# A hybrid attention and mixture-of-experts step: the last expert pair's rows are summed in PSUM, and the gathers go ahead of them

## The reference

```python
expert_id = g_sel[:, None] * EXPERTS_PER_GROUP + top_i          # two experts per token
gates = jnp.sum(jax.nn.one_hot(expert_id, N_EXPERTS) * top_w[..., None], axis=1)
a = jnp.einsum('nd,edf->nef', ht, w_gate)
u = jnp.einsum('nd,edf->nef', ht, w_up)
y = jnp.einsum('nef,efd->nd', jax.nn.silu(a) * u * gates[:, :, None], w_down)
x = layer_norm(ALPHA * x + gate * y, w, b)                      # gate: a row of the modulation
```

## Time and profile before

| what | us |
|---|---|
| median of 3 runs (1205.51 to 1209.25) | 1208.18 |
| the profiled execution's own time | 1204.98 |
| its span | 1203.1 |
| TensorE matmuls busy (fp32; two records for each) | 1047.1 (87%) |
| VectorE busy | 432.8 (36%) |
| ScalarE busy | 209.3 (17%) |
| POOL busy | 181.7 (15%) |
| mean granted TensorE clock | 0.928 |

### The profile page before, as it was taken

The page is one execution under the profiler, slowest core; times in us unless marked ns, Lnnn a source line. Parts: engine busy times, 40 slices in busy tenths (PEclk is TensorE's granted clock), DMA queues, the critical chain, the costliest instruction groups (busy, mean ns, idle before and its releaser), DMA issues.

```text
span 1203.1 us, 16527 instructions
## 1 busy us (share of the span) xinstructions
PE 1047.1 (87%) x6588; PEld 699.1 (58%) x6589; DVE 432.8 (36%) x1016; ACT 209.3 (17%) x524; POOL 181.7 (15%) x176
## 2 busy tenths in 40 slices
PE   4899999989979999887729999999896999998840
PEld 1766878568655555554328567775685655555420
DVE  0034545257741212100164344443686212211117
ACT  0322334100111111101102232421001111111000
POOL 0441020051111111101113000201312111111001
PEclk8899999999879999989859999999995999999985
DMA  8997222685999999999869312237858899999961
GB/s 353 249 270 238 70 84 71 226 293 241 348 419 418 419 419 419 418 420 419 331 210 320 106 67 80 103 112 281 320 213 340 332 416 419 419 418 419 412 260 60
DMA packets 102993, 343.83 MB, mean 286 GB/s; under 512 B 20530, under 2 KB 61538, under 8 KB 70404
## 3 DMA queue, kind: packets, MB, share of 16 engines
q1 hardware_dynamic: 88832, 316.58, 68.9%
q0 software_dynamic: 12352, 16.74, 4.6%
q10 hardware_dynamic: 1732, 9.45, 2.0%
HBM read 341.92 MB, written 26.16 MB: 306 GB/s over the span
## 4 chain that ended last, share of the span: by engine, by line
PE 69%; DMA 17%; DVE 4%; issue 4%; POOL 3%; ACT 2%; SPq 1%; POOLq 0%; DVEq 0%; ACTq 0%
PE ps L980 16%; PE ps L1254 15%; PE ps L973 8%; PE ps L1157 7%; PE ps L1278 7%; DMA ring<-in_exp_w_gate 5%; PE ps L1226 3%; DMA tables<-in_exp_w_gate 3%; DMA small<-in_exp_w_down 2%; DMA ring<-in_exp_w_down 2%; DMA ring<-in_w_mod 2%; PE ps L922 1%; PE ps L1073 1%; DMA arena<-token_rows,arena 1%; PE ps L1219 1%
## 5 line engine op out<-in xcount | busy, mean ns | idle before, releaser
L1254 PE MATMUL ps<-ring,arena 128*64 128x256 f32 x1488 | 211.0, 401 | 14.8 <-DMA ring<-in_exp_w_up 8.6
L980 PE MATMUL ps<-ring,arena 128*128 128x256 f32 (+1 forms) x960 | 200.1, 367 | 5.8 <-ACT arena L1488 5.8
L980 PEld LDWEIGHTS ps<-ring,arena 128*128 128x128 f32 x960 | 170.3, 195 | 28.7 <-issue 8.6
L1254 PEld LDWEIGHTS ps<-ring,arena 128*64 128x64 f32 x1488 | 129.7, 144 | 67.0 <-issue 26.2
L2050 DVE TENSOR_TENSOR arena<-arena,ps 128x256 f32<-128x256 f32 x32 | 13.5, 421 | 248.6 <-PE ps L1254 141.2
L973 PE MATMUL ps<-arena,ring 128*128 128x384 f32 x288 | 96.9, 490 | 0.7 <-ACT arena L1493 0.5
L1278 PE MATMUL ps<-ring,arena 128*64 128x512 f32 x304 | 80.3, 598 | 10.8 <-DMA ring<-in_exp_w_down 7.3
L1157 PE MATMUL ps<-ring,arena 128*128 128x256 f32 x384 | 87.9, 391 | 0.0
L1157 PEld LDWEIGHTS ps<-ring,arena 128*128 128x128 f32 x384 | 75.4, 198 | 10.8
L2236 POOL DMA_INDIRECT arena<-token_rows,arena x32 | 33.4, 1044 | 274.9 <-PE ps L1226 150.1
L1254 PE MATMUL ps<-arena 128*64 128x256 f32 x320 | 73.3, 382 | 1.9 <-DMA ring<-in_exp_w_up 1.7
(11 more groups left out here) (268 smaller groups left out, 1331.7 us busy)
## 6 DMA issues: line engine op xcount, KB each, us to landing
ring<-in_exp_w_up SPq DMA_DIRECT2D x51, 1024.0 KB, 24.2
ring<-in_exp_w_gate SPq DMA_DIRECT2D x46, 1024.0 KB, 22.6
ring<-in_w_mod SPq DMA_DIRECT2D x45, 1024.0 KB, 5.5
ring<-in_exp_w_down SPq DMA_DIRECT2D x40, 1024.0 KB, 27.3
ring<-in_w_in SPq DMA_DIRECT2D x24, 1024.0 KB, 13.3
arena<-in_exp_w_down SPq DMA_DIRECT2D x10, 1024.0 KB, 25.0
arena<-in_exp_w_gate SPq DMA_DIRECT2D x10, 1024.0 KB, 23.8
arena<-in_exp_w_up SPq DMA_DIRECT2D x10, 1024.0 KB, 25.2
```

Source lines behind the costliest of these rows:

```text
L980: mm = pe.matmul(out[:, 0:w], hT[:, ch, where * P:(where + 1) * P], unit(l, name)[:, ch, 0:w], start=(ch == 0), stop=(ch == CH - 1))
L1254: mm = pe.matmul(ps[64 * w:64 * w + 64, 2 * (i % 2) + kind, 0:FF], xgT[i % 2][:, ch, w * SLOTS:(w + 1) * SLOTS], weights[:, ch * FF:(ch + ...
```

## The change

- **Order.** Down 14 moves from after up 15 to directly after the turn of hidden 14, ahead of pair 15. Its weights move in the same way, and then come `gate2`, the last down weights, and `ln2`. The `gath` units reserve three ring places for the gathers.
- **Pair 15 is not scattered.** Its 128 rows are multiplied with the gate row on the way out of PSUM (`gate_last`), and TensorE adds them to the tokens with a matrix of gate weights (`marks_of_last`, `add_last`). `gate_weights` makes those weights and sets the weights of gathered rows that were not scattered to zero. The DRAM table is filled with zeros once, in layer 0, by eight POOL transfers of 384 KB.
- **Gathers.** ScalarE issues them during pair 15, once the scatters up to pair 14 have landed. ScalarE scales the first row and VectorE does the rest, alpha times x included (`add_choices`). TensorE copies this sum into PSUM (`add_former`).
- **Items** are single experts with 128 slots instead of pairs with 64, so three weight units are loaded instead of six. Their rows are not scattered either, but added in PSUM. An item starts after the last pair's rows have been read out.
- **The norm** takes its statistics and its first pass from PSUM. The moments of the tiles run ahead of the last passes.

```diff
 USE_ORDER = []
 for _i in range(PAIRS):
     USE_ORDER += [("pair", _i, _kind, _w) for _kind in range(2) for _w in range(2)]
-    if _i:
+    if _i and _i < PAIRS - 1:
         USE_ORDER += [("pair", _i - 1, 2, _w) for _w in range(2)]
-USE_ORDER += [("pair", PAIRS - 1, 2, _w) for _w in range(2)]
+    if _i == PAIRS - 2:
+        USE_ORDER += [("pair", _i, 2, _w) for _w in range(2)]
+LAST_DOWN = [("pair", PAIRS - 1, 2, _w) for _w in range(2)]
+GATH = [("gath", _t) for _t in range(TILES)]
+USE_ORDER += LAST_DOWN
+EXPERT_LOADS = USE_ORDER[:-2] + [("late", "gate2")] + GATH + LAST_DOWN + [("late", "ln2")]
+EXPERT_RELEASES = USE_ORDER[:-2] + GATH + LAST_DOWN + [("late", "gate2"), ("late", "ln2")]
...
-                if l:
-                    for t in range(TILES):
-                        sp.wait_ge(gathered[t].sem, gathered[t].at(l - 1, 16))
                 small_loads(l)
...
+                    if unit[0] == "late":
+                        load_late(l, unit[1])
+                    elif unit[0] != "gath":
+                        load(l, unit)
                 wait_alone(sp, items_known, items_known.at(l, 1))
                 o1 = items_before(sp, l + 1)
                 o0 = items_before(sp, l)
                 with sp.If(o1 > o0):
                     with sp.Fori(o0, o1) as i:
                         load_item(l, o0, i)
-                late_loads(l)
...
+                            if i == PAIRS - 1 and n == 1 and j == 0 and w == 0:
+                                mm.then_inc(down_half.sem, 1)
...
+            def add_former(l, t):
+
+                pe.wait_ge(presummed.sem, presummed.at(l, t + 1))
+                for n in range(2):
+                    pe.matmul(ps[:, FINAL_BANKS[t][n], :], ident, x[:, t, 512 * n:512 * n + 512], start=True, stop=False)
+
+            def add_last(l, t):
+
+                pe.wait_ge(last_rows.sem, last_rows.at(l, 1 + min(t, 1)))
+                for n in range(2):
+                    mm = pe.matmul(ps[:, FINAL_BANKS[t][n], :], ptl[:, t, :], ybg[min(t, 1)][:, 512 * n:512 * n + 512],
+                                   start=False, stop=True)
+                mm.then_inc(final_ready.sem, 1)
...
-                    if i:
+                    if i and i < PAIRS - 1:
                         down(l, i - 1)
 ...
                     hidden_T(l, i)
+                    if i == PAIRS - 2:
+                        down(l, i)
+                    if i == LAST_STEP:
+                        marks_of_last(l)
...
+                pe.wait_ge(last_rows.sem, last_rows.at(l, 2))
+                pe.wait_ge(o_rows.sem, o_rows.at(i, 0))
                 pe.wait_ge(o_xr_in.sem, o_xr_in.at(i, 16 * (l + 1)))
-                pe.wait_ge(xt_dve.sem, xt_dve.at(l, PAIRS))
-                turn_half(xr[0], 0).then_inc(o_xt.sem, 1)
+                turn_half(xr[0], 0, 6).then_inc(o_xt.sem, 1)
+                pe.wait_ge(o_gw.sem, o_gw.at(i, 1))
+                turn_marks([ps[:, 5, t * P:(t + 1) * P] for t in range(TILES)]).then_inc(o_pt.sem, 1)
...
+                for t in range(TILES):
+                    pe.wait_ge(o_rows.sem, o_rows.at(i, 1 + min(t, 1)))
+                    for n in range(2):
+                        mm = pe.matmul(ps[:, FINAL_BANKS[t][n], :], pti[t], yig[min(t, 1)][:, 512 * n:512 * n + 512],
+                                       start=False, stop=False)
+                mm.then_inc(o_added.sem, 1)
...
+                add_former(l, 0)
+                add_former(l, 1)
                 down(l, PAIRS - 1)
+                add_former(l, 2)
                 with pe.If(o1 > o0):
                     with pe.Fori(o0, o1) as i:
                         item(l, o0, i)
+                for t in range(TILES):
+                    add_last(l, t)
 
...
+            def load_rows_back(l):
+
+                for k in range(2):
+                    wait_alone(act, rows_out[k], rows_out[k].at(l, rows_out[k].step))
+                for t in range(TILES):
+                    wait_released(act, *SPOT[l, ("gath", t)][2])
+                    act.dma_start(gath(l, t).rearrange("p k d -> p (k d)"),
+                                  rows[1 + 2 * t * P:1 + 2 * (t + 1) * P].rearrange("(p k) d -> p (k d)", k=2))\
+                        .then_inc(gathered[t].sem, 16)
+
+            def weigh_first(l, t):
+
+                act.wait_ge(gathered[t].sem, gathered[t].at(l, 16))
+                a = gath(l, t)[:, 0, :]
+                act.activation(a, a, ACT.Identity, scale=wtsm[:, 0, t:t + 1]).then_inc(scaled.sem, 1)
...
-                    if i:
+                    if i and i < PAIRS - 1:
                         rows_half(l, i - 1)
+                    if i == PAIRS - 1:
+                        load_rows_back(l)
                     copy_hidden_T(l, i)
+                    if i == PAIRS - 2:
+                        rows_half(l, i)
+                    if i == LAST_STEP:
+                        marks_of_last(l)
                 wait_alone(act, items_known, items_known.at(l, 1))
                 o1 = items_before(act, l + 1)
                 o0 = items_before(act, l)
-                rows_half(l, PAIRS - 1)
+                act.wait_ge(weights_masked.sem, weights_masked.at(l, 1))
+                for t in range(TILES):
+                    weigh_first(l, t)
                 with act.If(o1 > o0):
                     with act.Fori(o0, o1) as i:
                         item(l, i)
 
...
+                for n, half in enumerate(sums_of(t)):
+                    cols = slice(512 * n, 512 * n + 512)
+                    ins = dve.scalar_tensor_tensor(xt[:, cols], half, ln_s[:, t, 12:13], lnw[:, cols], ALU.subtract, ALU.mult)
+                chain.link(ins)
...
+            def gate_weights(l, chain):
...
+            def marks_of_last(l, chain):
...
+            def add_choices(l, t, chain):
+
+                a, b = gath(l, t)[:, 0, :], gath(l, t)[:, 1, :]
+                dve.wait_ge(scaled.sem, scaled.at(l, t + 1))
+                chain.link(dve.scalar_tensor_tensor(a, b, wtsm[:, 1, t:t + 1], a, ALU.mult, ALU.add))
+                chain.link(dve.tensor_tensor(a, a, late_tile(l, "gate2", min(t, 1)), ALU.mult))
+                dve.scalar_tensor_tensor(x[:, t, :], x[:, t, :], ALPHA, a, ALU.mult, ALU.add).then_inc(presummed.sem, 1)
+
+            def gate_last(l):
+
+                dve.wait_ge(rows_out[0].sem, rows_out[0].at(l, rows_out[0].step))
+                dve.wait_ge(rows_out[1].sem, rows_out[1].at(l, rows_out[1].step))
+                dve.wait_ge(down_half.sem, down_half.at(l, 1))
+                gate = [late_tile(l, "gate2", k) for k in range(2)]
+                dve.tensor_tensor(ybg[0][:, 0:512], ps[:, 5, :], gate[0][:, 0:512], ALU.mult)
+                dve.wait_ge(down_ready.sem, down_ready.at(l, PAIRS))
+                dve.tensor_tensor(ybg[0][:, 512:D], ps[:, 6, :], gate[0][:, 512:D], ALU.mult).then_inc(last_rows.sem, 1)
+                dve.tensor_tensor(ybg[1].rearrange("p (a b) -> p a b", a=2), ps[:, 5:7, :],
+                                  gate[1].rearrange("p (a b) -> p a b", a=2), ALU.mult).then_inc(last_rows.sem, 1)
+
+            def final_moments(l, t, chain):
+
+                dve.wait_ge(final_ready.sem, final_ready.at(l, t + 1))
+                for n, half in enumerate(sums_of(t)):
+                    ins = dve.bn_stats(ln_s[:, t, 6 * n:6 * n + 6], half)
+                spread(t, chain, var2, ins)
...
+                        gate_weights(l, chain)
+                        dve.wait_ge(weights_masked.sem, weights_masked.at(l, 1))
+                        marks_of_last(l, chain)
                 o1 = items_before(dve, l + 1)
                 o0 = items_before(dve, l)
-                rows_half(l, PAIRS - 1)
+                dve.wait_ge(gate2_in.sem, gate2_in.at(l, gate2_in.step))
+                for t in range(TILES):
+                    add_choices(l, t, chain)
+                gate_last(l)
                 with dve.If(o1 > o0):
                     with dve.Fori(o0, o1) as i:
                         item(l, o0, i)
-                for t in range(TILES):
-                    dve.wait_ge(gathered[t].sem, gathered[t].at(l, 16))
-                    a, b = gath[t][:, 0, :], gath[t][:, 1, :]
-                    if t == 0:
-                        dve.wait_ge(gate2_in.sem, gate2_in.at(l, gate2_in.step))
-                    chain.link(dve.tensor_scalar(a, a, wts[:, 0, t:t + 1], None, ALU.mult))
-                    chain.link(dve.scalar_tensor_tensor(a, b, wts[:, 1, t:t + 1], a, ALU.mult, ALU.add))
-                    dve.tensor_tensor(a, a, late_tile(l, "gate2", min(t, 1)), ALU.mult).then_inc(combined.sem, 1)
-                    dve.wait_ge(combined.sem, combined.at(l, t + 1))
-                    chain.link(dve.scalar_tensor_tensor(x[:, t, :], x[:, t, :], ALPHA, a, ALU.mult, ALU.add))
-                    moments(t, chain, var2)
-                    normalise(l, t, chain)
+                dve.wait_ge(o_added.sem, o_added.at(o1, 0))
```

(15 more changed lines are left out.)

359 lines of the change are left out of this document (190 added, 169 removed).

## The result

The changed kernel takes **1214.51 us** (median of 6 runs, 1211.49 to 1217.07) against 1207.93 before (6 runs beside them): a ratio of 1.0048, 95% interval 1.0028 to 1.0069. The change costs 6.6 us.

A forecast was written before the change was run, and what follows sets the result against it. TensorE bounds each layer's front, the weight stream the expert stage, then a tail follows. Layer 0 +10.6 and layer 1 -1.6 give +9.0 us on the median 1208.18: 1217 us, range 1202 to 1226.

The forecast's parts named there:

- the chain of waits: End of each layer's expert stage: scatter 14, gather, ScalarE scaling, VectorE presum, two identity products, then down 15; 20.8 us later in layer 0.
- Scatter and gather, layer 0: After down 14: scatter lands 8.0 us after issue, first gather 7.3 us after its own, further tiles 5 us apart.
- even split: Gather and SyncE's queued loads each get half the DMA engines: 5 us per tile, bounds 2.5 and 7.5.
- Identity products at half clock: TensorE adding presummed tiles 0 and 1 into PSUM before down 15: 3.4 us per tile, bounds 1.7 and 3.4.
- The item: Layer 0's one overflow item starts 20.8 us later, takes 18.4 us through its down product, then 14.8 to tile 0.
- Clock recovery in layer 1's front: Start of layer 1: of 2.9 us lost to TensorE's low clock, 1.7 comes back as the item ends earlier.
- Layer 1: Its expert stage and tail: down 15 ends 19.7 us later, tail shrinks from 37.7 to 16.5 us, net -1.6 us.
- Edits costed at nothing: Zeroing the rows, gate weights, marks, transposes, copies and SyncE's dropped wait: 0 us taken; uncovered zeroing would cost 7.5.
- No change: Rival: the gather gets full rate; layer 0 +6.7, layer 1 -5.3, net +1.4 us, 1209.6; chance 0.15.
- Faster: Rival: scatter 14 lands in about 3 us, pair 15's weights come last; net -9.5 us, 1198.7; chance 0.25.
- Slower still: Rival: the gather gets a third of the engines; layer 0 +16.6, layer 1 -0.5, net +16 us, 1224; chance 0.13.
- The signs that it named: Gathers issued at 574 and 1155, landings 5 apart; in layer 1 down 15 near 1176, first tile 633; VectorE tail 14 us.

## Why the prediction was right, point by point

The direction, the size (1217 against 1214.5) and the chain of waits came out; the explanation that it gave for layer 0's loss was incomplete, and the size of the total owes something to errors that cancel.

- **Scatter and gather, layer 0.** Scatter 8.8 us (I took 8.0), first landing 9.1 after its issue (7.3), then 4.9 apart (5.0). The even split at first is in the bytes, 1.90 and 1.86 MB. By the Trainium skill, "DMA: Bandwidth & Descriptors", "Queues, rings and completion order", the engines take turns between queues by packets, and a packet there holds several descriptors. The profile's own packets were 674 to 248, of 2.8 and 7.5 KB on average; whether they are the packets of that rule no view tells. So the even split is measured in bytes, and that it comes from the rule is not shown. Less the 1.5 us of the late start, down 15 is at 597.7, 3.1 later than I had it: this is the term of the sum that was mis-sized most, by the first landing (1.8 us) and the scatter (0.8) above all.
- **Identity products at half clock.** 3.75 and 3.57 us (3.4 taken), after 13.3 us of idle TensorE, at a granted clock of 0.50 and 0.53. Right.
- **The item.** Start to end of its down product 18.3 us (18.4), and from there to tile 0 14.7 (14.8). Both right. But I costed "one item" only by its delay, and never asked what covered it before. The runs show what that is worth: 14.1 us before, 26.2 after, a difference of 12.1 (11.3 by the means) where the change loses 6.6. Putting the gathers ahead is worth as much, 12.5. My sum had the size, as it went row by row from the old end of tile 0 to the new one, but it named the gather alone as the cause, and the rivals left the item out.
- **Clock recovery in layer 1's front.** 1.7 us taken. The front took 0.2 less, and its first 32 records 9.57 us instead of 9.81 (6.92 at full clock): TensorE had rested for only 2.95 and 2.64 us before them and was slow all the same. Mis-sized by 1.5.
- **Layer 1.** -1.6 forecast, -2.4 measured up to VectorE's end. Down 15 is 18.3 later (19.7) and the tail after its start 20.7 us. The end of the last store, 2.0 shorter, was not in the sum.
- **Edits costed at nothing.** The zeroing: the first expert product of layer 0 comes at 346.2 to 348.9 in the profiles with it and 347.4 to 347.7 in the two without (the kernel before, and down 14 alone); nothing is seen. The move of down 14 was costed at nothing too. Made alone it put down 15 of layer 1 5.2 us later in the profiled execution, while the medians leave room for anything from 0 to 5. In the changed kernel down 15 waits for the gathers' sums and not for up 15, which should cover it; no run tests that.
- **The sum.** Layer 0: +10.6 forecast, +15.0 in the profiles (15.2 less 0.2), 3.1 of the gap from the gather and 1.5 from the clock. Layer 1: -1.6 forecast, -4.4 with the store. Together +9.0 against +10.6, and against +6.6 in the medians, so the errors of the layers partly cancelled, and the executions' spread of some 5 us did the rest. That 1217 came within 3 us is in part luck.
- **Rivals.** "No change" needed the gather at full rate: an even split was measured. "Faster" needed a scatter of 5 us; 8.8. Its picture, the gathers ahead of the last weights, was made true by another edit and gave 1202.05 where it had said 1198.7. "Slower still" was not met.
- **The signs that it named.** With the 1.5 and 16.5 us taken off by which the changed kernel's expert stages start later, the gathers went out at 575.1 and 1154.7 (574 and 1155), down 15 of layer 1 came at 1174.6 (1176), tile 0 of layer 1 at 636.5 (633), and VectorE's last stretch was 13.3 us with no gap over 1 us (14). The landings were 4.9 apart in layer 0 but 3.7 in layer 1 (5 and 3.5 in the sum).

## What to carry to other kernels

Before a step is moved out of a tail, list what runs beside that tail: here about 9 of the item's 27 us were hidden behind pair 15's scatter, and taking that scatter away left the item bare. A transfer that is moved into a full stream did best here in the stream's own queue, at the place where it is needed and ahead of all that is needed later. Where an in-order engine is given a wait, look for the next stage's first instruction behind it.
